# A hybrid decoder layer on one core: the order of VectorE's work at the border between two blocks of the recurrent pass

## What is computed

```python
def step(state, inp):
    r_t, w_t, k_t, v_t, a_t, b_t = inp
    sa = jnp.einsum('bhij,bhj->bhi', state, a_t)
    state = (state * w_t[:, :, None, :]
             + sa[..., :, None] * b_t[..., None, :]
             + v_t[..., :, None] * k_t[..., None, :])
    y = jnp.einsum('bhij,bhj->bhi', state, r_t)
    return state, y
```

```python
pf = pf + (token_shift(pf) - pf) * mu
```

## Time and profile before

| | |
|---|---|
| median of 3 runs | 2912.44 us (2911.47 to 2914.87) |
| the profiled execution | 2913.32 us, of which the span of the core is 2911.6 us |
| TensorE matmul busy | 2801.9 us, 96% of the span |
| TensorE weight load busy | 2327.5 us, 80% |
| VectorE busy | 1560.3 us, 54% |
| ScalarE busy | 1096.5 us, 38% |
| GpSimd busy | 477.5 us, 16% |
| mean granted TensorE clock | 0.985 |

### The profile page before, as it was taken

How to read it: one execution, slowest core, us unless ns; L and a number is a source line. 1 busy time by engine, 2 the same in 40 slices (tenths; PEclk the granted TensorE clock), 3 DMA queues, 4 the chain that set the end, 5 groups by cost and what they waited for, 6 DMA issues and landing times.

```text
span 2911.6 us, 75522 instructions
## 1 busy us (share of the span) xinstructions
PE 2801.9 (96%) x30981; PEld 2327.5 (80%) x30981; DVE 1560.3 (54%) x3137; ACT 1096.5 (38%) x2531; POOL 477.5 (16%) x627
## 2 busy tenths in 40 slices
PE   7999999999799999999999999999999999999996
PEld 6777777777588888888888888888888888888884
DVE  2421121121366666666666666666666666666664
ACT  3333333232133333344433333344443343344442
POOL 3201101101111211111111211111111211111210
PEclk8999999999899999999999999999999999999997
DMA  8622322322100000010000000000000000001000
GB/s 340 238 74 99 115 87 93 108 99 67 66 9 23 24 23 23 24 38 24 28 26 23 23 24 23 23 31 31 24 30 24 23 24 23 24 26 35 23 16 23
DMA packets 68707, 153.09 MB, mean 53 GB/s; under 512 B 3977, under 2 KB 37342, under 8 KB 66398
## 3 DMA queue, kind: packets, MB, share of 16 engines
q1 hardware_dynamic: 63134, 130.08, 12.9%
q0 software_dynamic: 1680, 11.01, 0.9%
q10 hardware_dynamic: 3632, 7.87, 0.7%
HBM read 98.61 MB, written 50.33 MB: 51 GB/s over the span
## 4 chain that ended last, share of the span: by engine, by line
PE 52%; DVE 11%; ACT 6%; issue 5%; DVEq 0%; DMA 0%; ACTq 0%
PE bank L928 26%; PE bank L977 12%; PE bank L964 8%; PE bank L1096 2%; DVE SV L1455 2%; DVE LA L1480 1%; ACT sig L1167 1%; ACT sig L1166 1%; DVE mix L1371 1%; PE bank L938 1%; DVE t L1400 1%; ACT UV L1257 1%; DVE LA L1476 1%; DVE kk L1407 1%; DVE t L1408 1%
## 5 line engine op out<-in xcount | busy, mean ns | idle before, releaser
L928 PE MATMUL bank<-xT,w 128*128 128x128 f32 x8704 | 1106.6, 281 | 7.4 <-DMA xT<-xt_dram 7.4
L928 PEld LDWEIGHTS bank<-xT,w 128*128 128x128 f32 x8704 | 1011.9, 192 | 43.5 <-issue 8.5
L1199 ACT ACTIVATE XX<-bank 128x256 f32<-128x256 f32 x320 | 123.0, 384 | 910.3 <-PE bank L977 897.9
L347 PE MATMUL bank<-xT,w 128*128 128x256 f32 x2048 | 448.6, 381 | 4.8 <-ACT xT L467 4.8
L347 PEld LDWEIGHTS bank<-xT,w 128*128 128x128 f32 x2048 | 391.6, 191 | 65.4 <-issue 10.5
L1465 DVE TENSOR_TENSOR XV<-bank,level_mask 128x256 f32<-128x256 f32 x320 | 132.9, 423 | 327.4 <-PE bank L977 318.1
L964 PE MATMUL bank<-wo,Y 128*128 128x512 f32 x512 | 233.5, 600 | 4.6 <-DVE Y L1425 4.6
L379 PE MATMUL bank<-wo,yc 128*128 128x512 f32 x512 | 226.5, 596 | 4.5 <-DVE yc L698 4.5
L977 PEld LDWEIGHTS bank<-XX,AI 64*64 64x64 f32 x5120 | 163.6, 136 | 63.5 <-issue 52.0
L671 DVE TENSOR_SCALAR gate<-gate 128x1024 f32<-128x1024 f32 x16 | 11.1, 694 | 368.0 <-ACT gate L487 368.0
L977 PE MATMUL bank<-XX,AI 64*64 64x64 f32 x5120 | 185.8, 222 | 4.6 <-DVE XX L1498 4.6
(11 more groups left out here) (182 smaller groups left out, 3588.2 us busy)
## 6 DMA issues: line engine op xcount, KB each, us to landing
x_in<-in_x SPq DMA_DIRECT2D x16, 1024.0 KB, 7.5
xr<-in_x SPq DMA_DIRECT2D x32, 512.0 KB, 4.4
xt_dram<-xT SPq DMA_DIRECT2D x32, 512.0 KB, 8.6
h_dram<-xr SPq DMA_DIRECT2D x32, 512.0 KB, 2.6
xT<-xt_dram SPq DMA_DIRECT2D x32, 512.0 KB, 3.3
gate_row<-h_dram SPq DMA_DIRECT2D x32, 512.0 KB, 3.3
out<-gate_row SPq DMA_DIRECT2D x32, 512.0 KB, 2.6
w<-in_w_in POOLq DMA_DIRECT2D x8, 1088.0 KB, 11.0
```

What stands on the lines that cost most here:

```text
L347: last = nc.tensor.matmul(bank[t // 2][:, (t % 2) * T1:(t % 2 + 1) * T1], w1[:, k, t * P:(t + 1) * P], xT[:, k, :], start=(k == 0), stop=( ...
L928: last = nc.tensor.matmul(bank[b][:, q * P:(q + 1) * P], w2[:, k, (t0 + q) * P:(t0 + q + 1) * P], xT[par][:, k, :], start=(k == 0), stop=( ...
L1199: s(nc.scalar.activation(XX[j][:, k].rearrange(flat), bank[2 + j][:, 256 * k:256 * (k + 1)], ACT.Copy), xx_ready, hold=False)
```

## The change

VectorE's queue at the end of a block is put in another order. `new_state` is cut in two. `state_sum(j)` adds chunk j's products to the state, and `new_state(j, steps, ready)` multiplies by the decay. For chunk 0 both still follow each other. For chunk 1 the sum stays where it was. The shift of the values comes right behind it, and the replaced key behind that. The product with the decay goes into the next block, behind LA and ahead of dend, under a signal of its own (`carried_ready`). On TensorE the bonus products no longer wait for the state; the grams wait for the sum (`sum_ready`), since they write the bank that it reads, and `from_state(0)` waits for the product.

```diff
-                    def new_state(j):
+                    def state_sum(j):
                         s.wait(y_ps, j + 1)
                         for e in range(2):
                             h = half(e)
-                            s(nc.vector.tensor_tensor(stmp[h], per_head(bank[7][h, 0:256]), SV[e][h], ALU.add), hold=bool(e))
+                            s(nc.vector.tensor_tensor(stmp[h], per_head(bank[7][h, 0:256]), SV[e][h], ALU.add),
+                              sum_ready if e and j else None, hold=bool(e) or j > 0)
+
+                    def new_state(j, steps, ready):
                         for e in range(2):
                             h = half(e)
-                            s(nc.vector.tensor_tensor(SV[e][h], stmp[h], dend[h, :, j:j + 1].broadcast_to([HD, NP, HD]), ALU.mult),
-                              s_ready if e else None, hold=bool(e))
+                            steps(nc.vector.tensor_tensor(SV[e][h], stmp[h], dend[h, :, j:j + 1].broadcast_to([HD, NP, HD]), ALU.mult),
+                                  ready if e else None, hold=bool(e))
...
+                        if not first:
+                            new_state(NC - 1, pv, carried_ready)
                         s(nc.vector.tensor_copy(dend[:, :, :].unsqueeze(3), chunks(sig[:, 0])[:, :, :, C - 1:C]), hold=False)
...
-                        new_state(1)
-                        if ahead:
+                        state_sum(1)
+                        if ahead:
+                            shift(n + 1, 3)
                             replaced_key()
-                            shift(n + 1, 3)
...
                         else:
                             variance()
-                            pv.wait(s_ready, NC)
                         bonus_sum()
...
                         s.wait(lhs_ready, 1)
+                        if not first:
+                            pv.wait(sum_ready, 1)
...
                         s.wait(la_ready, j + 1)
+                        if j == 0 and not first:
+                            pv.wait(carried_ready, 1)
```

More of the change, by code:

```diff
@@ L61 @@
 HEAD_DVE = 9
-DVE_OWN = 14
+DVE_OWN = 12
 LN_MAX = 1e19
@@ L784, in build @@
             tail_act = signal("tail_act", 1)
-            tail_dve = signal("tail_dve", 2 * NP)
+            tail_dve = signal("tail_dve", 2 * NP + 1)
             group_ps = signal("group_ps", 5)
@@ L835, in build @@
             r_ready = signal("r_ready", NC)
-            s_ready = signal("s_ready", NC)
+            s_ready = signal("s_ready", 1)
+            sum_ready = signal("sum_ready", 1)
+            carried_ready = signal("carried_ready", 1)
             v_ready = signal("v_ready", 1)
@@ L1001, in inverses, with from_state @@
                                 other(i - 2)
-                    def from_state(j):
+                    def from_state(j, first=False):
                         s.wait(la_ready, j + 1)
+                        if j == 0 and not first:
+                            pv.wait(carried_ready, 1)
                         if j:
@@ L1102, in run @@
                         inverses(fill, (lambda h: None) if first else out_half)
-                        from_state(0)
+                        from_state(0, first)
                         if ahead:
@@ L1528, in run @@
                             clamp(0)
-                        new_state(0)
+                        state_sum(0)
+                        new_state(0, s, s_ready)
                         if ahead:
```

## The result

The changed kernel takes 2864.93 us (median of 4 runs, 2863.39 to 2867.66) against 2912.61 us before: a ratio of 0.9837, interval 0.9822 to 0.9851. It is 47.7 us faster. The forecast was 2879 us, 33.5 us faster, with a range that ended at 2874: the direction and the mechanism hold, the size does not. The term that was too small is the cost of a stop of TensorE. A second set of five runs gave 2867.42 us.

A forecast was written before the change was run, and what follows sets the result against it. TensorE was taken as the bound, standing still at block borders; 17 plain borders at 0.96 us and 14 back edges at 1.34 - 0.1 gave 33.7 us, from 2912.4 to 2879 us, range 2874 to 2900.

The forecast's parts named there:

- What bounds the kernel: Second pass: TensorE works 64.55 of 65.50 us and 64.61 of 65.96 us per block; its standing time is the gain.
- Shift ahead of the key: VectorE's queue at a plain border: the shift starts about 1778.25 and ends about 1779.38, in place of 1784.02.
- The product with the decay: VectorE pair moved behind LA: stall beside GpSimd taken as 0, up to 0.2 us, at most 0.95; pair costs 0.9 us.
- The first rival: The 0.95 us stall moves to the shift or kk on VectorE; 13.6 us gained, 2899 us; chance 0.12.
- The bonus products: TensorE at a plain border: they follow the variance at once, at 1783.22, and the 0.85 us are gone.
- The grams: TensorE behind its transposes: grams start 0.96 us sooner at a plain border, 1.34 us sooner at a back edge.
- The charge for VectorE at a back edge: VectorE takes the first gram 0.15 to 0.2 us late, with 0.19 us of room; 0.1 us charged.
- VectorE's wait of 0.3 us for the first gram: Sign in the profile after: VectorE waits some 0.3 us in plain blocks and not at all at back edges.
- The sum and the ceiling: 17 x 0.96 + 14 x (1.34 - 0.1) = 33.7 us; ceiling all TensorE idle time, 35 us, 2877 us.
- Slower: VectorE's queue at the block's start becomes the bound through two stalls; 14 us slower, 2927 us; chance 0.05.
- the passed wait: TensorE stands at the transposes for rs, BK or rg instead, giving everything back; 2912 us; chance 0.05.
- theory A: For bonus products made to wait for LA: a stop costs 0.26 us beside its idle row; 2943 us.

The follow-up runs named there:

- GpSimd later: The kernel before, with GpSimd's two BK products made to wait until the state's product is written: 2936.37 us, ratio 1.0081.
- the product alone: The changed kernel with the shift behind the key again, so that only the product with the decay moves: 2897.89 us, ratio 0.9949.
- the product further back: The changed kernel with the state's product and dend behind the first level of the inverse: 2860.97 us, ratio 0.9821; repeated, 2861.91 us.
- the shift alone: The kernel before, with the shift of the values ahead of the replaced key and nothing else changed: 2909.63 us, ratio 0.9985.
- The kernel that waits for LA: The changed kernel, with the bonus products made to wait for LA: 2975.88 us, ratio 1.0221.

## Why the prediction was wrong

By its own steps, in order:

- *What bounds the kernel* held: TensorE, and its stops at the borders. The only other change in a block is how late VectorE takes the gram, below.
- *Shift ahead of the key.* Forecast to start 0.3 us behind the sum and to run in 1.13 us; it starts 0.27 us behind it and takes 1.13 us. Right.
- *The product with the decay.* Forecast that the stall vanishes; every one of its instructions now takes 416 to 424 ns. Right, and the runs with GpSimd later and with the product alone show the cause. The first rival had the stall moving on to the shift or kk. No run shows that: with the key right behind the sum, as in the kernel with the product alone, kk takes 0.73 us and t takes the stall.
- *The bonus products.* This is the step that failed. I took the idle row of 0.85 us for the cost of the stop, and an end by the profile plus a gap for the next start. The group ahead of a stop ends by the profile 0.15 us later than the point at which the next one could start, and the group behind it took 0.11 us longer. From start to start, and with the group behind it, the stop cost 1.11 us (1.00 and 0.11).
- *The grams.* The same mistake again, ahead of the grams, where the plain border has hardly any idle row: 0.96 us forecast for both stops together, 1.41 measured (65.51 less 64.10). At a back edge 1.34 us forecast for the grams and 1.86 measured as TensorE's own part (65.96 less the 64.10 of a plain block).
- *The charge for VectorE at a back edge* was 0.1 us; it is 0.31 us (64.41 against 64.10), and some 0.03 us in plain blocks. I had the gram taken 0.15 to 0.2 us late with 0.19 us of room behind it. Late it was by 0.2 us, but for other reasons: the 0.53 us at the branch, which I had carried over, is gone, and TensorE arrives 0.4 us sooner than I thought, which used up the spare time. VectorE's wait of 0.3 us for the first gram, forecast as a sign at plain borders, did not come for the same reason. That the charge was too small by 0.2 us and not by more is partly luck, since the term was built on two wrong inputs. The kernel with the product further back gives the charge back.
- *The sum and the ceiling.* For the 30 whole blocks the terms give 16 x 0.96 + 14 x 1.24 = 32.7 us; measured were 43.6. Two stops at each border, each 0.22 to 0.26 us more than their rows, are 14 us; VectorE's lateness takes 3 back. That is 11 of the 11 us. The "ceiling" of 35 us was none, because busy time by the profile contains the price of the stops: 64.55 us fell to 64.11. Another 4 us lie at the end of the program, in and behind the last block; the forecast had nothing for them beyond its one border, and their cause is open.
- *Slower, and the passed wait*: neither came. rs was in time.

So the mechanism and its order were right, and one term, the cost of a stop of TensorE, was too small by about a quarter of a microsecond, twice at each of the 31 borders. Why a stop costs that much more was not tried and stays open. What the traces show beside it is that the first weights of a group are loaded ahead where the engine runs through and not behind a stop. After, the first weights of the bonus products are loaded 0.42 us before their matmul; before, both start at the same time, 1784.07:

```profile
1827.03 0.19 PEld L954 LDWEIGHTS bank<-rk,rk_sum 128*128 128x128 f32 x1 [0.24 <-issue]
...
1827.45 1.05 PE L954 MATMUL bank<-rk,rk_sum 128*128 128x128 f32 x8
```

## What to carry to other kernels

Cost a wait of TensorE from start to start, against the same two groups at a place where they follow each other without a stop; the idle row leaves out the overlap that a stop breaks, here a quarter of a microsecond for each. Look in the queue of a helping engine for the instruction that nobody waits for soon, and for the one whose input has long been there: here they were the state's product and the shift. They paid 48 us together and 20 apart: with the shift alone the stop only went over to the next group that waits for VectorE. And when an instruction of VectorE is stretched beside GpSimd, moving it pays only where the next one in the queue doesn't inherit the stall.

## What the runs showed of the hardware

In this kernel the granted clock fell behind most stops of 2.1 us and behind none of 1.65 us. Before, with stops of 0.85 us, a block's clock is 1.00. The kernel with GpSimd later stops for 1.65 us at each plain border and keeps 1.00:

```profile
1529.93:1596.23 66.30, 64.55 (x879) 55.48 (x878) 44.29 (x91) 26.73 (x65) 11.51 (x14) 1.00 0.08 26
```

The kernel that waits for LA stops for some 2.1 us at each border and drops from 2.4 to 1.2 GHz for between three and four microseconds in 26 of its 30 blocks. In the block shown the drop begins some 1.6 us after TensorE has gone on, in others sooner. The four blocks that kept 1.00 have the same stop of 2.12 or 2.13 us; what decides between them no run shows. Its granted clock in stretches of 2 us around the stop at 1542.4 to 1544.5, and the groups of that border:

```profile
1544.00:1546.00 2.00, 1.52 (x22) 1.40 (x24) 1.69 (x5) 0.00 (x0) 0.00 (x0) 1.00 0.18 74
1546.00:1548.00 2.00, 2.00 (x44) 1.88 (x38) 0.36 (x1) 0.60 (x1) 0.00 (x0) 0.52 0.00 0
1548.00:1550.00 2.00, 2.00 (x28) 2.00 (x27) 0.07 (x1) 1.19 (x2) 0.00 (x0) 0.63 0.00 0
1550.00:1552.00 2.00, 2.00 (x26) 1.88 (x23) 1.90 (x4) 0.00 (x0) 0.00 (x0) 1.00 0.03 8
```

```profile
1545.57 1.58 PE L1080 MATMUL bank<-center,mix 128*64 128x64 f32 x32
1547.08 1.12 PE L1093 MATMUL bank<-ident,BK 64*128 64x64 f32 x16
1547.98 2.73 PE L1102 MATMUL bank<-LA,BK 64*128 64x128 f32 x32
```

Those groups took 1.15, 0.71 and 2.00 us in the changed kernel. The drop costs 1.5 us per block (67.96 against 66.46), 39 us over the 26 blocks that have it, which more than covers the 33 us by which this kernel came out above theory A's estimate. The estimate had the stop at the back edges at 2.6 us, 0.5 longer than it is, 7 us over the 14, which is about the difference.
